# Weight buffers and the operands XH and XL moved to 64 bytes past a multiple of 128

## The reference

```python
px = (rmsnorm(x, norm1_g[l]) * (1.0 + sc1) + sh1) @ w_in[l] + b_in[l]
...
x = x + g1 * (y_x @ w_out[l])
x = x + g2 * swiglu(rmsnorm(x, norm2_g[l]) * (1.0 + sc2) + sh2, w_gu[l], w_down[l])

def swiglu(h, w_gu, w_down):
    gate, up = jnp.split(h @ w_gu, 2, axis=-1)
    return (jax.nn.silu(gate) * up) @ w_down
```

## The kernel before, in words

| tensors | first byte before | modulo 128 (256) before | modulo 128 (256) after |
|---|---|---|---|
| raw0 to raw3, w_lo0 to w_lo3 (the same memory) | 16512, steps of 4096 | 0 (128) | 64 (192) |
| w_hi0, w_hi1 | 32896, 36992 | 0 (128) | 64 (192) |
| Z, TH, X | 41088, 53376, 57600 | 0 | 64 |
| ident, ones, word | 56512, 57024, 57536 | 64 | 0 |
| XH, XL | 82176, 106752 | 0 (0) | 64 (64) |
| XH2, XL2 | 98560, 114944 | 0 (0) | 64 (64) |
| HH, HL | 149184, 173760 | 64 (192) | 64 (64) |
| YH2, YL2 | 143808, 160192 | 64 (192) | 64 (64) |
| PH, PL | 208320, 212416 | 64 (192) | 64 (64) |
| PWH, PWL | 198080, 189888 | 64 (192) | 64 (64) |
| ZS | 206272 | 64 | 64 |

## Time and profile before

### The profile page before, as it was taken

One profiled execution on the slowest core, in us unless ns is written; L12 is line 12 of the kernel. 1 busy time (PEld: TensorE's weight loads), 2 busy tenths in 40 slices (PEclk: granted clock), 3 DMA queues, 4 the chain that ended last, 5 costly groups with the idle time before them and its releaser, 6 DMA issues.

```text
span 2586.4 us, 39643 instructions
## 1 busy us (share of the span) xinstructions
PE 2522.5 (98%) x14594; PEld 2083.7 (81%) x14594; DVE 1386.4 (54%) x2065; ACT 776.3 (30%) x1620; POOL 1544.1 (60%) x1625
## 2 busy tenths in 40 slices
PE   6999999999999999999999999999999999999999
PEld 4888988888888886888788887778888888777876
DVE  5864556742853758726433333444444545556754
ACT  3224353111111123244321212222222222443544
POOL 3433245765766665543777777776666676556563
PEclk9999999999999999999999999999999999999999
DMA  7341142332333322121233232433333333323231
GB/s 280 107 155 41 34 179 86 127 130 65 122 130 98 119 60 69 58 66 42 83 96 94 93 98 82 130 106 100 91 103 96 93 103 94 98 73 98 83 106 65
DMA packets 79264, 255.57 MB, mean 99 GB/s; under 512 B 9872, under 2 KB 13712, under 8 KB 78864
## 3 DMA queue, kind: packets, MB, share of 16 engines
q1 hardware_dynamic: 63136, 213.21, 25.8%
q10 hardware_dynamic: 15984, 40.40, 5.1%
HBM read 236.28 MB, written 2.10 MB: 92 GB/s over the span
## 4 chain that ended last, share of the span: by engine, by line
PE 88%; DVE 4%; issue 3%; POOL 2%; ACT 2%; DMA 1%; SPq 0%; ACTq 0%; POOLq 0%; DVEq 0%
PE PS L463 21%; PE PS L466 21%; PE PS L464 21%; PE PS L1668 4%; PE PS L1670 4%; PE PS L1669 4%; PE PS L725 1%; POOL w_lo L444 1%; PE PS L714 1%; PE PS L708 1%; DMA raw<-in_wout 1%; PE PS L1524 1%; POOL w_hi L442 1%; DVE Z L2425 1%; DVE XL L2432 1%
## 5 line engine op out<-in xcount | busy, mean ns | idle before, releaser
L444 POOL TENSOR_TENSOR w_lo<-raw,w_hi 128x512 fp32r<-128x512 f32 (+1 forms) x606 | 880.5, 1453 | 50.6
L463 PE MATMUL PS<-XH,w_hi 128*128 128x512 f32 (+1 forms) x2080 | 782.7, 376 | 16.5 <-DVE XL L2432 3.3
L464 PE MATMUL PS<-XL,w_hi 128*128 128x512 f32 (+1 forms) x2080 | 755.6, 372 | 0.0
L466 PE MATMUL PS<-XH,w_lo 128*128 128x512 f32 (+1 forms) x2080 | 707.2, 373 | 0.0
L437 POOL TENSOR_TENSOR word<-ones 128x1 f32<-128x1 f32 x303 | 93.7, 309 | 869.4 <-PE PS L466 544.2
L463 PEld LDWEIGHTS PS<-XH,w_hi 128*128 128x128 f32 x2080 | 392.2, 189 | 118.6 <-issue 9.3
L442 POOL TENSOR_SCALAR w_hi<-raw 128x512 fp32r<-128x512 f32 (+1 forms) x606 | 482.0, 795 | 0.0
L464 PEld LDWEIGHTS PS<-XL,w_hi 128*128 128x128 f32 x2080 | 392.4, 189 | 70.0
L466 PEld LDWEIGHTS PS<-XH,w_lo 128*128 128x128 f32 x2080 | 362.5, 188 | 55.1
L1668 PE MATMUL PS<-XH,w_hi 128*128 128x512 f32 (+1 forms) x640 | 230.9, 361 | 8.4 <-DVE XL L2432 8.4
L1670 PE MATMUL PS<-XH,w_lo 128*128 128x512 f32 (+1 forms) x640 | 224.9, 351 | 0.0
(11 more groups left out here) (346 smaller groups left out, 3507.0 us busy)
## 6 DMA issues: line engine op xcount, KB each, us to landing
raw<-in_wgu SPq DMA_DIRECT2D x88, 512.0 KB, 3.5
raw<-in_wa SPq DMA_DIRECT2D x80, 512.0 KB, 3.5
modt<-in_wmod SPq DMA_DIRECT2D x48, 512.0 KB, 9.9
raw<-in_win SPq DMA_DIRECT2D x48, 512.0 KB, 3.5
modv<-in_wmod ACTq DMA_DIRECT2D x48, 512.0 KB, 4.7
raw<-in_wdn SPq DMA_DIRECT2D x32, 512.0 KB, 3.6
QS<-Z ACTq DMA_DIRECT2D x96, 128.0 KB, 2.6
raw<-in_wout SPq DMA_DIRECT2D x16, 512.0 KB, 3.5
```

What stands on the lines that cost most here:

```text
L444: pool.tensor_tensor(lo, src, hi.bitcast(FP32), ALU.subtract).then_inc(s_split, 1)
L463: pe.matmul(acc(s)[:, a:b], hi, rh[:, i, a:b], start=i == 0, stop=False)
L464: pe.matmul(acc(s)[:, a:b], hi, rl[:, i, a:b], start=False, stop=False)
L466: last = pe.matmul(acc(s)[:, a:b], lo, rh[:, i, a:b], start=False, stop=i == k - 1)
```

## The change

Two unused tensors of 64 bytes per partition are placed, one ahead of raw0 and one behind XL. All that is placed between them lies 64 bytes higher, all that is placed behind the second lies 128 bytes higher. Instructions and their order stay.

```diff
+        place("lead", [P, 16])
         raw = [place(f"raw{i}", [P, KT * P]) for i in range(RING)]
         w_hi = [place(f"w_hi{i}", [P, KT, P], FP32R) for i in range(2)]
         w_lo = [place(f"w_lo{i}", [P, KT, P], FP32R, addr=addr_of[f"raw{i}"]) for i in range(RING)]
...
         XH = place("XH", [P, KT, T], FP32R)
         XL = place("XL", [P, KT, T], FP32R)
 
+        place("lead2", [P, 16])
         tri = place("tri", [P, 2, P])
```

## The result

The changed kernel takes 2594.93 us (median of 5 runs, 2594.07 to 2595.32) against 2585.69 (2584.41 to 2588.71): the ratio is 1.0034 with a 95% interval of 1.0023 to 1.0045, some 9 us slower. The forecast of 2564 has the wrong sign, and the time lies above the range.

What follows compares the result with a forecast made beforehand. The prediction took PE's matmul pace to bound the kernel. From 2586.4 us it took 22 us for XH and XL (20 at 512 columns, 2 at 256) and nothing for other parts, giving 2564, range 2541 to 2591.

Steps and rivals of the forecast that it cites:

- What bounds the kernel: Whole kernel: PE is busy 2522.5 of 2586.4 us, so the pace at which matmuls follow each other sets the time.
- Part 1: XH and XL matmuls: moving both to 64 past a multiple of 128 saves 22 us, 3.3 ns per 512-wide matmul.
- Part 2: Weights w_hi, w_lo (over raw) moving too: no gain or loss, from PH rows at 226.4 and 232 ns a matmul.
- Parts 3 and 4: X, Z, TH moving, and POOL's splits and DMAs into moved buffers: nothing; POOL has 0.65 us left per tile.
- The rival of the distance: Pace follows distance between weights and moving operand; XH keeps its pace, HH and YH slow to it: 2592.5 us, chance 0.15.
- The address is not the cause: All matmuls: the operand's address does not separate the paces, so no effect, 2586 us; chance 0.20.
- The fast rhythm: 512-wide matmuls, both operands at 64, settle at PH's fast rhythm of 226.5 ns: 20 us more saved, 2544; chance 0.17.

Runs made afterwards that it cites:

- The first half of the change: Only the unused piece of 64 bytes ahead of raw0 was added to the kernel before: 2585.96 us, ratio 0.9995.
- mixed distances: Three kernels, against the kernel before, putting one k-step's operands at different distances between weights and moving operand: 2587.24, 2580.63 and 2581.96 us.

## Why the prediction was wrong

*What bounds the kernel* was right: with the same instructions the time followed the pace of the matmuls, in both directions, from 2561.84 to 2598.73 us. PE's idle time stayed as it was: span less PE's busy time is 63.9 us before, 63.6 in the changed kernel, and 61.3 to 66.4 in the others.

*Part 1 is the step that failed.* It read 3.3 ns from HH against XH and ascribed them to the operand's own place, "the contrast that the change makes for XH and XL". But in those rows the weights stand in one place, so an operand's place and its distance from the weights are the same thing there; the rows cannot tell them apart. The change moves XH and the weights together, and the distance stays 128. The first half of the change shows that own places cost nothing. With the weights moved alone by 64, the matmuls with XH and XL take 23 us less by their starts, about the 22 of the forecast, although XH has not moved: the price was near, the cause was not. The sum also left HH and YH as they were, and they are what lost: 6.6 us with HL and YL.

*Part 2 let the warning go.* The two runs of PH, 226.4 and 232 ns, were averaged to 229, and an average between two rhythms was taken for no gain or loss from the weights. They have distance 0, where a long stream settles at 0.680 a step (226.7 ns a matmul) and one that has just been entered often does not: XH's first four steps at 0 take 0.690 each with the weights moved by 128, and YH's mean step at 0 is 0.683, with single steps up to 0.70. The fast run of twelve had the settled pace; why it had it from its first gap is not shown. Used as an argument against the distance ("has distance 0 and is as slow as XH"), the short run misled a second time.

*Parts 3 and 4* hold: DVE's busy time is 1389.7 us after 1386.4, ACT's 776.6 after 776.3. POOL's two splits at 64 take what they took at 0:

```profile
L446 POOL TENSOR_TENSOR w_lo<-raw,w_hi 128x512 fp32r<-128x512 f32 x574 | 843.5, 1469 | 48.0
L444 POOL TENSOR_SCALAR w_hi<-raw 128x512 fp32r<-128x512 f32 x574 | 459.6, 801 | 0.0
```

*The rival of the distance* was right in sign, in place and in what counts, the place of the one operand against the other (as a rule for single matmuls it fails with mixed distances), and near in size: it had 6 us, and the interval of the ratio holds 6 to 12. The profiles show 6.6 us for HH and YH. It got 0.15 and the range ended below it, at 2591; with one contrast that two theories explain equally, they should have had like chances, and the range should have held both. *The address is not the cause* fell in each run that moved a distance: the steps changed with nothing but places. The Trainium skill, "SBUF — State Buffer", Specifications (TRN2), gives lines of 16 bytes. By such lines alone all multiples of 32 bytes would be alike; the trace does not agree, with steps of 0.682, 0.700 and 0.687 us at distances 0, 32 and 64. *The fast rhythm* exists, at distance 0 and 512 columns, but the change does not bring it about; at 768 columns the same distance gives 1.053 and is no gain on 1.052.

## What to carry to other kernels

Where matmuls follow one another without waits, place the stationary and the moving operand by their distance: in this kernel 64 or 0 modulo 256, the better of them by the width that is streamed, is worth up to 3% of a k-step (0.703 to 0.682 us). At 512 columns give all the operands of one step the same one of these two: none of the mixed steps came down to 0.687. Other types, and widths other than these two, were not run. Read a difference between two tensors' rows as a difference of everything that the tensors do not share, and move each side alone before pricing a move of both. Padding ahead of one buffer shifts all buffers behind it; the loss here came from two operands that the change's name did not mention.

## What was not expected of the hardware

The pace of fp32r matmuls of 512 columns depends on where two operands lie relative to each other, between 226.7 and 234 ns each at a granted clock of 0.996 to 0.998 in the mean of a profile, with both at multiples of 32 bytes. Its dependence on the distance is not monotonic: 0.682, 0.700, 0.687, 0.700, 0.698, 0.703, 0.700, 0.700 us a step from 0 to 224. The best distance depends on what is streamed: 0 is best at 512 columns (0.682 us) and no gain at mixed 512 and 256 (1.053 us, against 1.040 at 64). And the step is not a sum over single matmuls: at 512 columns four of the five mixed cases miss it by 5 to 8 ns.
